# A decoder trunk on one core: the dense layer's tile waits, the attention block's mask and exponentials, and one program block in place of four

## What is computed

```
x = x + even_mixer(rms_norm(x), ...)      # gated DeltaNet and a short convolution
x = x + swiglu(rms_norm(x), w1, w3, w2)   # dense, inner width 3584
x = x + odd_mixer(rms_norm(x), ...)       # 16 query heads, 2 key/value heads of 64, window 128, sinks
x = x + moe_swiglu(rms_norm(x), ...)      # top 2 of 8 experts, inner width 3584 each

def swiglu(h, w1, w3, w2):
    return (silu(h @ w1) * (h @ w3)) @ w2

# attention, per block of 128 queries, over the keys of this block and the one before
s = where(band, q @ k.T * 64 ** -0.5, -1e30)
m = maximum(max(s), sink)
p = exp(s - m)
o = (p / (sum(p) + exp(sink - m))) @ v
```

## Time and profile before

| | |
|---|---|
| median of 3 runs | 1572.93 us (1572.63 to 1580.54) |
| profiled execution | 1571.26 us, of which the span of the profile is 1569.4 us |
| PE busy | 1492.5 us (95% of the span) |
| DVE busy | 1166.3 us (74%) |
| ACT busy | 944.5 us (60%) |
| mean granted TensorE clock | 0.971 of full speed |

### The profile page before, as it was taken

How to read it: one execution, slowest core, us unless ns; L and a number is a source line. 1 busy time by engine, 2 the same in 40 slices (tenths; PEclk the granted TensorE clock), 3 DMA queues, 4 the chain that set the end, 5 groups by cost and what they waited for, 6 DMA issues and landing times.

```text
span 1569.4 us, 19375 instructions
## 1 busy us (share of the span) xinstructions
PE 1492.5 (95%) x7334; PEld 1251.7 (80%) x7334; DVE 1166.3 (74%) x998; ACT 944.5 (60%) x819; POOL 36.4 (2%) x21
## 2 busy tenths in 40 slices
PE   6999889999997889999999999999999999999997
PEld 5998667777786678888888888888888888888885
DVE  4869444444457638988898888898898889888884
ACT  5642342433345335777677777777677677777773
POOL 0000000000000000000000000000000000100000
PEclk9999899999998689999999999999999999999998
DMA  9501345545423317999999999999999999999993
GB/s 332 210 7 63 126 151 207 178 160 182 165 97 123 108 48 270 359 377 362 391 385 365 387 386 368 381 376 365 377 395 369 370 380 383 380 389 368 382 381 97
DMA packets 185244, 439.51 MB, mean 280 GB/s; under 512 B 5872, under 2 KB 7152, under 8 KB 185200
## 3 DMA queue, kind: packets, MB, share of 16 engines
q1 hardware_dynamic: 180320, 426.29, 73.5%
q0 software_dynamic: 2704, 9.96, 2.4%
q10 hardware_dynamic: 2176, 2.65, 0.5%
HBM read 432.60 MB, written 6.29 MB: 280 GB/s over the span
## 4 chain that ended last, share of the span: by engine, by line
PE 51%; issue 7%; DMA 3%; DVE 1%; ACT 1%; POOL 0%; ACTq 0%; SPq 0%; DVEq 0%; POOLq 0%
PE ps L256 16%; PE ps L258 16%; PE ps L257 16%; DMA raw<-in_od_moe_w 2%; PE ps L442 1%; DMA out<-arena,slot_tok 1%; ACT whi L239 0%; DVE wlo L245 0%; PE ps L1789 0%; PE ps L1798 0%; PE ps L1781 0%; PE ps L319 0%; PE ps L1807 0%; POOL out L1489 0%; ACT arena L1528 0%
## 5 line engine op out<-in xcount | busy, mean ns | idle before, releaser
L245 DVE TENSOR_TENSOR wlo<-raw,whi 128x2048 fp32r<-128x2048 f32 (+1 forms) x408 | 910.3, 2272 | 197.4 <-ACT whi L239 195.8
L239 ACT CAST whi<-raw 128x2048 fp32r<-128x2048 f32 (+1 forms) x408 | 753.5, 1899 | 180.6 <-DMA raw<-in_od_moe_w 99.5
L256 PE MATMUL ps<-whi,hThi 128*128 128x512 f32 (+1 forms) x1248 | 494.5, 396 | 18.7 <-DVE aTlo L1004 8.0
L258 PE MATMUL ps<-whi,hTlo 128*128 128x512 f32 (+1 forms) x1248 | 487.0, 390 | 0.0
L257 PE MATMUL ps<-wlo,hThi 128*128 128x512 f32 (+1 forms) x1248 | 486.7, 390 | 0.0
L256 PEld LDWEIGHTS ps<-whi,hThi 128*128 128x128 f32 x1248 | 236.4, 189 | 69.5 <-issue 15.6
L258 PEld LDWEIGHTS ps<-whi,hTlo 128*128 128x128 f32 x1248 | 235.7, 189 | 49.5
L257 PEld LDWEIGHTS ps<-wlo,hThi 128*128 128x128 f32 x1248 | 236.5, 189 | 46.3
L256 PE MATMUL ps<-whi,aThi 128*128 128x512 f32 x560 | 219.4, 392 | 1.4 <-DVE aTlo L434 1.4
L258 PE MATMUL ps<-whi,aTlo 128*128 128x512 f32 x560 | 218.2, 390 | 0.0
L257 PE MATMUL ps<-wlo,aThi 128*128 128x512 f32 x560 | 217.8, 389 | 0.0
(11 more groups left out here) (272 smaller groups left out, 830.6 us busy)
## 6 DMA issues: line engine op xcount, KB each, us to landing
raw<-in_od_moe_w SPq DMA_DIRECT2D x168, 2048.0 KB, 9.3
raw<-in_ev_ffn_w SPq DMA_DIRECT2D x21, 2048.0 KB, 7.8
raw<-in_ev_w_in SPq DMA_DIRECT2D x7, 2048.0 KB, 11.0
raw<-in_ev_w_out SPq DMA_DIRECT2D x2, 2048.0 KB, 8.3
raw<-in_od_w_in SPq DMA_DIRECT2D x2, 2048.0 KB, 7.8
raw<-in_od_w_out SPq DMA_DIRECT2D x2, 2048.0 KB, 10.7
xres<-in_x SPq DMA_DIRECT2D x1, 1024.0 KB, 6.1
xres<-in_x ACTq DMA_DIRECT2D x1, 1024.0 KB, 4.9
```

Source lines behind the costliest of these rows:

```text
L239: act.copy(whi[s][:, part], raw[s][:, part]).then_inc(hi_ready, 1)
L245: dve.tensor_tensor(wlo[s][:, part], raw[s][:, part], whi[s][:, part].bitcast(F32), ALU.subtract).then_inc(lo_ready, 1)
L256: pe.matmul(to, lhi, rhi, start=first, stop=False)
L258: return pe.matmul(to, llo, rhi, start=False, stop=last)
```

## The change

In words, with the line numbers of the changed kernel where they differ:

- **One block.** The four stages' lists are joined into one `nc.Block()` (`even_sync`, `dense_sync` and so on are called one after another). The engines no longer meet between stages. Apart from what follows, the instructions and their order stay.
- **Dense stage.** `up(w1)` waits for tile t's bank just ahead of tile t's matmuls, in place of both ahead of the first. The first transposed product goes to ps[6:8], which are idle then (`FIRST_TURN`), and PE makes it after `up(w1)` of the next column block, not before it. On ACT the hi split of unit `u0 + 2` is moved ahead of the first silu; in the loop the order on ACT is as it was.
- **Attention stage.** The mask is added on PE: it and the identity are rounded into the idle `aThi` (`mask_r`, `ident_r`), and each bank of scores begins with identity times mask, 256 or 512 columns wide. The scale 64**-0.5 goes into the root of the query norm. DVE takes its maxima straight from PSUM (two reductions and one operation), and ACT makes the exponentials straight from PSUM. For tile 1 the second half of the transposed probabilities is copied by ACT (`turned_late`) in place of DVE. `turn_q` of the first eight heads is moved between the two tiles of c = 2, and that of the last eight behind turn(0); the first two maxima are taken ahead of the query norm of c = 2. ACT's split of unit `U_OUT1 + 1` is moved: its halves go behind the first `take_turned` and behind exps(1).
- **Output product.** It goes tile by tile (tile 0 with both units, then tile 1) in place of unit by unit. Tile 0's attention output is transposed during j = 6, tile 1's after the first product. The transposes of `xres` stand in the middle of the last product. The helper `added` gives the counts that fit the new order of the additions.

Shown without its white space, and cut:

```diff
+        def added(n, h, t):
+            signal, before = ADDED[n]
+            return signal, before + (2 * t + h if n == 3 else 2 * h + t) + 1
 # dense, ACT
             act.wait_ge(rs_ready, 1)
+            split_hi(act, u0 + 2, 2, n0)
             act_silu(act, TT, u0, 0)
 # dense, PE
-                def up(u, s, to):
+            def up(u, s, to, free=None):
                 for t in range(TT):
+                    if free is not None:
+                        pe.wait_ge(aTlo_ready, free + t + 1)
                     ins = tokens_by_columns(pe, u, to[t][:, :], t, s=s)
             up(u0 + 1, 1, H3)
-                turn(0)
             def step(i, first=False):
                 pe.wait_ge(sil_ready, 2 * i)
-                    pe.wait_ge(aTlo_ready, 2 * i)
-                    up(w1, 2, H1)
+                up(w1, 2, H1, None if first else 2 * i - 2)
                 pe.wait_ge(a_ready, 2 * i)
+                if first:
+                    turn(0, FIRST_TURN)
                 up(w3, 0, H3)
 # attention, ACT
-                        x = prob[j % 2][:, at:at + keys]
-                        act.activation(x, x, ACT.Exp, bias=nmax[t][:, hh:hh + 1],
+                    act.activation(prob[j % 2][:, to:to + keys], ps[2 * (j % 2) + h % 2][:, at:at + keys], ACT.Exp,
+                                   bias=nmax[t][:, hh:hh + 1], accum_out=rsum[t][:, hh:hh + 1])
+            def turned_late(j):
+                act.wait_ge(pT_ps, j + 1)
+                act.wait_ge(av_ps, j - 1)
+                act.copy(probT[j % 2][:, 4:8, :], ps[5][:, :].rearrange("p (c i) -> p c i", c=4))
 # attention, DVE
-                        link(dve.scalar_tensor_tensor(x[:, 2 * b:2 * b + 2], s, HD ** -0.5, over_heads(m, 2),
-                                                      ALU.mult, ALU.add))
-                    link(dve.tensor_reduce(smax[t][:, hs]..., x..., AX.X, ALU.max))
-                    link(dve.tensor_tensor(smax[t][:, hs], smax[t][:, hs], sinks[:, hs], ALU.max))
-                    dve.tensor_scalar(nmax[t][:, hs], smax[t][:, hs], -1.0, None, ALU.mult).then_inc(neg_max, 1)
+                for b in range(2):
+                    x = ps[2 * (j % 2) + b][:, 0:2 * keys].rearrange("p (h k) -> p h k", h=2)
+                    dve.tensor_reduce(smax[1][:, hs]...[:, b], x, AX.X, ALU.max).then_inc(dve_step, 1)
+                dve.scalar_tensor_tensor(nmax[t][:, hs], smax[1][:, hs], -1.0, neg_sinks[:, hs], ALU.mult, ALU.min)
 # attention, PE
+                for b in range(2):
+                    pe.matmul(ps[2 * (j % 2) + b][:, 0:2 * keys]..., ident_r, over_heads(m, 2), start=True, stop=False)
-                                        kT[rows, hh // GRP, 0:keys], start=True, stop=True)
+                                    kT[rows, hh // GRP, 0:keys], start=False, stop=h >= 2)
+                if j == 6:
+                    turn_out(0)
                 values(j)
+            project_out(0, 0, range(KD)).then_inc(out_ps, 1)
+            turn_out(1)
+            project_out(1, 0, range(KD)).then_inc(out_ps, 1)
+            project_out(0, 1, range(KD)).then_inc(unit_used, 1)
+            project_out(1, 1, range(KD // 2))
             pe_turn_x(pe, 3, 0)
+            project_out(1, 1, range(KD // 2, KD)).then_inc(unit_used, 1)
```

More of the change, by code:

```diff
@@ L236, in split_hi @@
                 act.wait_ge(unit_used, u - NS + 1)
-            for h in range(2):
+            for h in halves:
                 part = slice(h * size // 2, (h + 1) * size // 2)
@@ L1414, in slots_of @@
             return Psel[:, t, :]
[L1416 to L1432 removed]
+        out_t = out[0].rearrange("(t p) d -> p t d", p=P)
```

2380 lines of the change are left out of this document (1208 added, 1172 removed).

## The result

The changed kernel takes 1536.97 us (median of 4, 1534.25 to 1540.36) where the kernel before took 1572.95 on the same chip (median of 4, 1572.63 to 1580.54): a ratio of 0.9769, 95% interval 0.974 to 0.9798. The unaltered changed kernel, timed again later in five executions, gave 1538.92 (1533.97 to 1542.78); over all nine executions the median is 1538.65, which lies inside the range. So about 2 us of the surplus over the forecast is spread, and the rest has to be found in the trace.

The account below looks back on a forecast made before the run. PE was taken to bound the expert stage, with waits and half clock costing time elsewhere; 8.0 + 5.8 + 2.8 + 3.4 + 0.7 + 8.0 = 28.7 us off 1571.26 gave 1543 us towards the median, range 1537 to 1554.

Parts of the forecast that it names:

- I take full clock from 524 on: Attention core: PE's granted clock is full from 524 us on, so the output product starts at 543.6, not 554.75.
- Dense loop: Dense stage: five PE stops of 1.61 us for tile 1's split vanish at the ends of passes, gain 8.0 us.
- First turn: Dense stage, first transposed product: PE waits of 0.84 and 4.99 us vanish, 5.8 us, plus 2.8 us of half clock.
- Borders: Without meetings between stages: even to dense gains 3.4 us, dense to attention 0.7 us; third border counted in the attention end.
- Attention core: turn(0) some 4 us earlier, scores(2) not, shorter DVE waits; output product at 543.6 in place of 554.75.
- The page's rule: Attention core: sustained busy time brings full clock from about 510, product near 539; the forecast said the trace disagrees.
- Stage end: Output product to router: 32.1 us against 28.95 before, with a new 4.0 us stall at the transposes of `xres`.
- Experts, 0: Expert stage: PE sets it and the change leaves it alone; as long as before, within 1 us.
- load limit: Rival, 5 in 100: expert loads lose rate; at 3% no change, from 3.7% slower, at 4% 1582 us.
- dense rival: Rival, 6 in 100: a moved wait returns in the dense stage, losing half of 16.6 us, giving 1551 us.
- the best clock case: Rival, 15 in 100: full clock from the attention core's first steps, product at 538.2, total 1536 to 1538 us.

Follow-up runs that it names:

- two of the others: Changed kernel with its stages in four blocks again, 1545.77 us; changed kernel with the first transposed product back ahead of the next `up(w1)`, in H1's banks, 1548.31 us.
- the late kernel: Changed kernel with the transposes of tile 0's attention output behind values(7), not during j = 6: 1547.66 us, ratio 0.9846.
- the one with the copy on DVE: Changed kernel with the second half of tile 1's transposed probabilities copied by DVE again, not by ACT: 1542.19 us, ratio 0.9813.
- filled gap and addition together: Changed kernel plus 17 unread wide matmuls ahead of turn(0), and the third `xres` addition ahead of DVE's lo split: 1528.54 us, repeated 1531.36.
- the kernel with the loop's wait back: Changed kernel with the dense loop's old wait for both tiles' splits ahead of `up(w1)`: 1548.51 us, ratio 0.9844.

## Why the prediction was right in kind and short in size

The forecast's terms for the waits held. The step that failed is in the attention core: "I take full clock from 524 on", with the output product at 543.6. That term was to give 11.15 us and gave 15.8 in the first profile and 13.4 in the second. The dense loop's term was 1.6 us too small beside it. That the first median lies 0.03 us outside the range is chance; the surplus of some 6 us over 28.7 is not.

- **Dense loop, 8.0 us forecast, 9.6 measured.** The mechanism is right: five stops, gone. What failed is the size of one, 1.61 us. This is the idle time from the modelled end of the matmul before, but matmuls overlap. The rows had the right number: from 274.36 to 276.36 is 2.00 us start to start where it should be 0.23, so 1.77, and the first step behind the stop (276.36 to 276.69) takes 0.33 in place of 0.23. That makes 1.87, and 1.91 is measured by passes with and without the stop.
- **First turn, 5.8 and 2.8 for the clock.** No gap and no half clock there after. Undone alone it cost 7.8 us of its stretch, with a second gap of 4.39 and not 4.99, since the wait stayed tile by tile; with these 0.6 it is 8.4 of the 8.6 forecast. Right.
- **Borders, 3.4 and 0.7.** The first dense product stands 2.0 us behind the start of the addition (2.01 or 2.02 in all kernels of one block), before 4.57: 2.6 us for the 2.7 forecast. From there to K's transposes it is 254.0 us, before 274.07, a gain of 20.1 where the forecast had 18.0 (its 0.7 for the slow first matmuls included): 1.6 of the difference are the loop's stops, and 0.5 are not accounted for.
- **Attention core, 11.15 us forecast, 15.8 in one profile and 13.4 in the other.** The order of events is right: turn(0) 4.4 us earlier, scores(2) 0.8, stops at the values of tile 1 under 1 us. The stop at the values of j = 3, 1.32 us in the first profile and 1.58 in the second, was not foreseen. Wrong is the sentence "I take full clock from 524 on". That is 41.6 us behind K's transposes; measured were 30.0 and 34.5 us in the unaltered kernel, and 40.6 and 40.5 in two of the others. In these last two the core took 59.2 us against the 61.2 of the forecast: so 2 us are mostly prices set a little high (scores(2) 23.7 us behind K for 24.3, a step 4.33 for 4.45, maxima 0.95 for 1.0), and the other 0.3 to 2.7 are the clock's return. Taking one instant for it was the mistake: before, one profile had shown one value, and nothing said how it varies. The argument for that instant was thin too: it leant on the clock that "stayed full" from 537.5 to 547.6 with 3.0 us of gaps, and left out that it had fallen for 6.8 us just before and fell again for 10.2 just behind, behind stops of 2.38 and 1.38 us. That the changed kernel's core had no such second fall in its first profile, and one of 3.4 us in its second, was luck as far as the forecast goes.
- **The page's rule.** By the Trainium skill, "TensorE: Matmul & The Clock Gate" (The two states you'll see), a short stretch of sustained busy time brings full clock. The forecast set it at 510 in the old time, 27.6 us behind K, with the product near 539. Half clock lasted to 30.0 us behind K in the first profile (56.5 us to the product, old time 538.97) and to 34.5 in the second, with PE busy for 8.21 of 10.2 and 13.81 of 17.1 us. The first lies near the rule's value, the second does not.
- **Stage end, −3.15 forecast, −3.4 measured.** The stall of 4.02 us at the named place, for the named reason, with half clock behind it, and 32.35 us from product to router against the 32.1 of the forecast. The experiment that moves the addition takes it away for 5.5 us.
- **Experts, 0.** Within the spread (983.5 to 987.8 us over the fifteen profiles of the changed kernel and of what was made of it). The load limit did not come; nor did the dense rival. Of the rivals, the best clock case (1536 to 1538 us) was nearest in time, but its ground, the wide matmuls, is not shown to be what did it.

What stays open is what sets the instant of the clock's fall, and with it that it comes back 30 us behind K in one profile and 35 or 41 in another, with the same instructions.

## What to carry to other kernels

Price a stop of PE from start to start, against the pace of its neighbours, not by its idle time; and where the clock has been at half, look for the stop ahead of it and price both together, since a moved wait, or filler in an idle bank, may be worth more than the stop (the filler here 5.6 us in the late kernel, nothing that shows in the changed one). Before a joined or reordered stage is trusted, follow every item that stands in a queue between a producer and its waiting consumer: one addition behind a 4.5 us split cost 5.5 us here and was free to move. And do not take the length of a half-clock stretch from a single profile.

## What the runs showed of the hardware

- Between two profiles of one kernel the half clock behind the same idle stretch of 4.1 us lasted 10.2 and 17.1 us; over the ten profiles with that stretch in the same place 10.2 to 23.9, the longer the earlier it began (19.7 to 16.6 us behind K). With the stretch filled by matmuls it was 0, 6.8 and 10.2.
- From j = 3 on, stops of some 1.5 us were followed by half clock: 13.7 us in the late kernel, 6.8 in the one with the copy on DVE, 3.4 behind the 1.56 us stop, and 3.4 behind the 1.6 us stop near 500 us in six kernels. It doesn't always follow. In the second profile of filled gap and addition together, a stop of 1.58 us (this row of PE) has only full clock behind it (this window). So has the stop of 1.59 us at the values of j = 3 in the kernel with the loop's wait back, and the five stops of 1.6 us in the dense loop never had any half clock.

```profile
499.95 0.77 PE L1399 MATMUL ps<-arena 128*128 128x64 f32 x5 [1.58 <-DVE arena L1266]
```

```profile
495.50:543.30 47.80, 44.01 (x274) 36.82 (x273) 24.82 (x41) 18.87 (x53) 0.34 (x1) 1.00 0.28 100
```
- A shorter half clock in the core was worth less than half its length: with 10.2 us of it and not 23.9, the core was 2.7 us shorter, where half of the difference is 6.8. At full clock PE reaches the values of j = 2 and 3 before DVE has copied, and stops for it (1.05 and 1.32 us, in the first profile).
